# Inverse transform of the long convolution with the spectra as stationary operand, in a fused float32 block pair

## The chip, the cores and the metric

The kernel runs on one core of one Trainium2 chip. The metric is the device time of one execution in microseconds (us). TensorE is called PE, its weight loads PEld, VectorE DVE, ScalarE ACT, GpSimd POOL, SyncE SP. Everything is computed in float32: most products go as three products of rounded parts (hi times hi, hi times lo, lo times hi), the transform below as plain float32 matrix products, which the chip splits in two records each.

## What is computed

Two blocks follow each other on 1024 tokens of 1024 channels: a Hyena block (long convolution and SwiGLU), then a block with gated linear attention and pooling. The change lies in the long convolution:

```python
z = short_conv(u @ w_in + b_in, conv_w, conv_b)
x0, x1, v = jnp.split(z, 3, axis=-1)
s = (v * x1).astype(jnp.float32)
g = hyena_filter(L, ...)
n = 2 * L
y = jnp.fft.irfft(jnp.fft.rfft(s, n=n, axis=1) * jnp.fft.rfft(g, n=n, axis=0)[None],
                  n=n, axis=1)[:, :L]
y = (y + s * skip.astype(jnp.float32)).astype(u.dtype) * x0
return y @ w_out + b_out
```

## The kernel before

Activations lie with channels on partitions, in 8 tiles of 128 channels by 1024 tokens. The Fourier transform of the convolution is split into a part over 16 positions and a part over 64 (of 128): 16 groups of spectra are multiplied and transformed back over the 16 positions in the stage "spec" (`inverse`, `spec_inverse`). Each of its 32 half steps ends with a copy of a result by ACT to `yi` (L1438) and a transfer of 256 KB from ACT's DMA queue into `YB` (L1441): even steps bring channels 0 to 511 (semaphore `yb_in[0]`), odd steps channels 512 to 1023 (`yb_in[1]`). `YB` is 128 partitions (64 frequencies, real and imaginary) by 16 positions by 1024 channels.

The stage "inv" does the rest, by a list `INV` of 24 jobs, each with one of the four PSUM tiles `ps` of 128 x 1024 in turn:

- a "rows" job (16 of them) multiplies the 128 x 64 matrix `idft`, as stationary operand, with 1024 columns of `YB` (L1233), in pieces of 512 columns for channels 0 to 511 (8 jobs) and of 256 columns for the others. The result has 64 partitions (time) and goes back into `YB` by an ACT copy (L1503).
- a "tile" job (8, one for each 128 channels) transposes those rows with 16 small transposes of 64 x 128 (L1238), so that channels are on partitions.

DVE then makes of each tile e: `y` = `ps` * `rn` + skip term (L1914), times the gate `G0` (L1919), and, one tile behind, the low part `A[:, 1, e]` (`y_lo_of`, L1904). ACT makes the skip term (`skip_of`, L1487) and the high part (`y_hi_of`, L1481). The output projection "wout" follows on PE (`panel_mm`, L1060): 8 jobs, each of 8 steps k of 6 products of 512 columns, and its first job waits at step k for the low part of tile k (`y_lo`).

The order on every engine is that of the program text; engines meet by semaphores. Before "inv", PE waits for `spec_ev`, the last copy to `yi`, and for `yb_in`. SP loads the block's input `X` (4 MB) again as soon as PE, ACT and DVE have ended "spec" (L943).

Of the kernel before, what the change touches and what calls it, by code (L numbers as in the profile page):

```python
# [20 lines left out]
ACT = mybir.ActivationFunctionType  # L21
# [3 lines left out]
P = 128  # L25
D = 1024
T = 1024
KT = D // P
# [10 lines left out]
N1, N2 = 128, 16  # L39
HALF = N1 // 2  # L40
GROUPS = 16
# [26 lines left out]

INV = [("rows", 0, 512, n2) for n2 in range(0, N2, 2)]
for _e in range(4):
    INV += [("rows", 512, 256, 4 * _e), ("tile", _e)]
INV += [("rows", 768, 256, 0), ("tile", 4)] + [("rows", 768, 256, _n2) for _n2 in (4, 8, 12)]
INV += [("tile", _e) for _e in (5, 6, 7)]


def inv_rows(e):

    return max(o for o, j in enumerate(INV) if j[0] == "rows" and j[1] <= 128 * e < j[1] + j[2])  # L80

PHASES = [("mlp0", 1, 0), ("zin0", 1, 1), ("norm1", 1, 0), ("zin1", 1, 1), ("mlp1", 1, 0), ("zin2", 1, 1),
          ("mlp2", 1, 0), ("zin3", 1, 1), ("zin4", 12, 12), ("mix", 40, 8), ("sfwd", 32, 0), ("tapnorm", 1, 0),
          ("spec", 0, GROUPS), ("inv", len(INV), 0), ("wout", 8, 8), ("first", 1, 1), ("norm2", 1, 0), ("second", 3, 3)]


UPS = [[(f"up{_p}", _n // 2)] for _p, _n in enumerate(FPARTS)]
# [11 lines left out]
J0, N0, A0 = {}, {}, {}  # L101
_j = _n_ = 0
for _name, _jobs, _pan in PHASES:
# [5 lines left out]
assert V_PANEL % 2 == 0 and HP % 2 == 0  # L109

_a = 0
AUX = {"norm1": 1, "mlp0": 1, "mlp1": 1, "mlp2": 1, "mix": 32, "tapnorm": 1, "sfwd": 32, "inv": len(INV), "norm2": 1,
       "normf": 1, "normc": 1, "lr": 1, "heads": HA * HEADS, "pool": 8, "norm4": 1}
for _name, _, _ in PHASES:
    A0[_name] = _a
# [29 lines left out]
def program(nc, d, out):  # L145

    ctx = ExitStack()
    with ctx:
# [38 lines left out]
        TT = [at(f"T{i}", [P, T], RT + 4 * K * i) for i in range(4)]  # L187
# [45 lines left out]
        YB = at("YB", [P, N2, T], RH)  # L233
# [41 lines left out]
        ps = [ctx.enter_context(nc.psum_tensor(f"ps{s}", [P, 2 * 512], F32)) for s in range(4)]  # L275
# [17 lines left out]
        panel_done, aux_done = sem("panel_done"), sem("aux_done")  # L293
        evac = [sem(f"evac{s}") for s in range(4)]
# [3 lines left out]
        def slot(phase, u):  # L298
            return (J0[phase] + u) % 4

        def turn(phase, u, i=0, per=0):

            return (J0[phase] + u) // 4 + i * (per // 4)
# [28 lines left out]
        n1, n2 = NormSems("mix", tiles=False), NormSems("ffn", tiles=False)  # L332
# [29 lines left out]
        yb_in = [sem("yb_in0"), sem("yb_in1")]  # L362
# [31 lines left out]
        def cc(name, rows=P):  # L394
            w = {"idft": 64, "tneg": 16, "tmask": 16}.get(name, 128)
            return cst[0:rows, CST[name]:CST[name] + w]

        ident, ones = cc("ident"), cc("ones")
# [640 lines left out]
        def _(pe):  # L1039
            mm = nc.tensor.matmul  # L1040

            def free(phase, u, i=0, per=0):

                q = turn(phase, u, i, per)
                if not (isinstance(q, int) and q == 0):
                    pe.wait_ge(evac[slot(phase, u)], q)
# [78 lines left out]
            with pe.Fori(0, 2) as i:  # L1125
                for q in range(4):
                    o, g = 5 * q, i * 4 + q
# [7 lines left out]
                    for u in range(2):  # L1135
                        p = begin(1 + u)
                        pe.wait_ge(hbs_made, g * 2 + (u + 1))
                        for c in range(2):
                            last = mm(p[:, c * 512:(c + 1) * 512], hbs[u][:, :], wtap[:, c * 512:(c + 1) * 512],
                                      start=True, stop=True)  # L1140
                        last.then_inc(aux_done, 1)
                    for u in range(2):
                        p = begin(3 + u)

                        pe.wait_ge(evac[slot("mix", o + 1 + u)], turn("mix", o + 1 + u, i, 20) + 1)
                        for c in range(2):
                            last = mm(p[:, c * 512:(c + 1) * 512], cc("dft_g"), tap[u][:, c * 512:(c + 1) * 512],
                                      start=True, stop=True)
                        last.then_inc(aux_done, 1)

            with pe.Fori(0, N2 // 2) as i:
                for u in range(2):
# [3 lines left out]
                    for e in range(KT):  # L1156
                        last = nc.tensor.transpose(ps[slot("sfwd", u)][0:HALF, e * P:(e + 1) * P], sn[u][:, e, :], ident)
                    last.then_inc(aux_done, 1)
                for u in range(2):
                    free("sfwd", 2 + u, i, 4)  # L1160
                    pe.wait_ge(evac[slot("sfwd", u)], turn("sfwd", u, i, 4) + 1)
                    for c in range(2):
                        last = mm(ps[slot("sfwd", 2 + u)][:, c * 512:(c + 1) * 512], cc("dft_s", HALF),
                                  st_[u][:, c * 512:(c + 1) * 512], start=True, stop=True)
# [3 lines left out]
            for e in range(KT):  # L1168
                last = mm(ps[slot("tapnorm", 0)][:, e:e + 1], gacc[:, e * P:(e + 1) * P], ones[:, 0:1],
                          start=True, stop=True)  # L1170
# [41 lines left out]
            for n in range(2 * GROUPS):  # L1212
                g, c = n // 2, n % 2
# [8 lines left out]
            pe.drain().then_inc(ended["pe"], 1)  # L1222

            pe.wait_ge(spec_ev, 2 * GROUPS)
            for o, (kind, *j) in enumerate(INV):
                p = ps[slot("inv", o)]
                free("inv", o)
                if kind == "rows":
                    c0, w, m0 = j
                    if m0 == 0:  # L1230
                        pe.wait_ge(yb_in[c0 // 512], 16 * GROUPS)
                    for u in range(T // w):
                        last = mm(p[0:HALF, u * w:(u + 1) * w], cc("idft"), YB[:, m0 + u, c0:c0 + w], start=True, stop=True)  # L1233
                else:
                    e, q = j[0], inv_rows(j[0])
                    pe.wait_ge(evac[slot("inv", q)], turn("inv", q) + 1)
                    for m in range(N2):
                        last = nc.tensor.transpose(p[:, m * HALF:(m + 1) * HALF], YB[0:HALF, m, e * P:(e + 1) * P],  # L1238
                                                   ident[0:HALF, 0:HALF])
                last.then_inc(aux_done, 1)  # L1240
            panel_jobs("wout", 2, A, ready=(y_lo, 0))
            project("first", 0, (n2.lo, 0))
# [35 lines left out]
            for g in range(4):  # L1278
# [6 lines left out]
                for m in range(2):  # L1285
                    free("pool", 6 * g + 4 + m)
                    for k in range(2):
                        pe.wait_ge(pd_made, 2 * g + k + 1)
                        for c in range(2):
                            last = mm(ps[slot("pool", 6 * g + 4 + m)][:, c * 512:(c + 1) * 512],  # L1290
                                      wpl[:, k, m * P:(m + 1) * P], pd[k][:, c * 512:(c + 1) * 512],
                                      start=(k == 0), stop=(k == 1))
# [9 lines left out]
        def _(act):  # L1302
            A_ = nc.scalar.activation
# [157 lines left out]
            for n in range(2 * GROUPS):  # L1461
                c = n % 2
# [16 lines left out]
            def y_hi_of(e):  # L1479
                act.wait_ge(y_made, e + 1)  # L1480
                A_(A[:, 0, e, :], TT[2 + e % 2][:, :], ACT.Copy).then_inc(y_hi, 1)  # L1481

            def skip_of(e):
                if e >= 2:
                    o = INV.index(("tile", e - 2))
                    act.wait_ge(evac[slot("inv", o)], turn("inv", o) + 1)
                A_(TT[e % 2][:, :], S[:, e, :], ACT.Copy, scale=vcol("skip", e)).then_inc(skip_made, 1)  # L1487

            def around(e):

                if e:
                    y_hi_of(e - 1)
                    if e + 1 < KT:
                        skip_of(e + 1)

            skip_of(0)
            skip_of(1)
            for o, (kind, *j) in enumerate(INV):
                if kind == "rows":

                    c0, w, m0 = j
                    act.wait_ge(aux_done, A0["inv"] + o + 1)
                    A_(YB[0:HALF, m0:m0 + T // w, c0:c0 + w], ps[slot("inv", o)][0:HALF, :].rearrange("p (a b) -> p a b", b=w),  # L1503
                       ACT.Copy).then_inc(evac[slot("inv", o)], 1)

                    if o and INV[o - 1][0] == "tile":
                        around(INV[o - 1][1])
                elif o + 1 == len(INV) or INV[o + 1][0] == "tile":
                    around(j[0])
            y_hi_of(KT - 1)  # L1510

            def residual_squares(ph, n, src, gain=None):
# [31 lines left out]
            for p, nf in enumerate(FPARTS):  # L1544
                last = p == len(FPARTS) - 1
# [17 lines left out]
            with act.Fori(0, 2) as i:  # L1563
                for u in range(4):
                    e = i * 4 + u
# [47 lines left out]
            with act.Fori(0, 2) as i:  # L1613
                for u in range(4):
                    e = i * 4 + u
# [5 lines left out]
            for g in range(4):  # L1621
# [4 lines left out]
                for u in range(2):  # L1626
                    s = slot("pool", 6 * g + u)
                    act.wait_ge(panel_done, N0["pool"] + 4 * g + u + 1)
                    A_(up[u][:, PAD:PAD + T], ps[s][:, :], ACT.Copy).then_inc(evac[s], 1)
                for m in range(2):  # L1630
                    s = slot("pool", 6 * g + 2 + m)
# [6 lines left out]
            with act.Fori(0, 2) as i:  # L1638
                for u in range(4):
                    e = i * 4 + u  # L1640
# [36 lines left out]
        def _(dve):  # L1677
# [137 lines left out]
            with dve.Fori(0, 3) as i:  # L1815
                ch.enter(i, 8 + 8 + 1)
                for u in range(4):
                    z_tile(slot("zin4", u), turn("zin4", u, i, 4) + 1, i * 4 + (N0["zin4"] + u),
                           i * 2 + (10 + 8 * (u % 2) + u // 2))
                    for j in range(2):  # L1820
                        m = 2 * u + j
# [9 lines left out]
                    n, e = i * 4 + (N0["zin4"] + u), i * 2 + (2 + u // 2)  # L1831
# [9 lines left out]
            with dve.Fori(0, 2) as i:  # L1841
                ch.enter(i, 16)
                for q in range(4):
                    o, g = 5 * q, i * 4 + q
                    z_tile(slot("mix", o), turn("mix", o, i, 20) + 1, g + N0["mix"], g)
                    for u in range(2):
                        s = slot("mix", o + 1 + u)
# [3 lines left out]
                    for u in range(2):  # L1851
                        s = slot("mix", o + 1 + u)
# [34 lines left out]
            for n in range(2 * GROUPS):  # L1887
                c = n % 2
# [16 lines left out]
                                 ).then_inc(y_lo, 1)  # L1905

            for e in range(KT):
                o = INV.index(("tile", e))
                s, y = slot("inv", o), TT[2 + e % 2]
                dve.wait_ge(skip_made, e + 1)  # L1910
                if e >= 2:
                    dve.wait_ge(y_lo, e - 1)
                dve.wait_ge(aux_done, A0["inv"] + o + 1)
                V_.scalar_tensor_tensor(out=y[:, :].rearrange("p (a b) -> p a b", b=N2),  # L1914
                                        in0=ps[s][:, :].rearrange("p (b a) -> p a b", a=HALF),
                                        scalar=rn[:, e:e + 1], in1=TT[e % 2][:, :].rearrange("p (a b) -> p a b", b=N2),
                                        op0=ALU.mult, op1=ALU.add).then_inc(evac[s], 1)
                dve.wait_ge(evac[s], turn("inv", o) + 1)
                V_.tensor_tensor(y[:, :], y[:, :], G0[:, e, :], ALU.mult).then_inc(y_made, 1)  # L1919
                if e:  # L1920
                    y_lo_of(e - 1)
# [350 lines left out]
```

## Time and profile before

| | us |
|---|---|
| median of 3 runs | 2643.86 |
| lowest and highest run | 2642.76, 2653.99 |
| span of the profiled execution | 2636.2 |
| stage "inv" on PE in it, first product to the first of "wout" | 635.3 to 674.7 |
| busy PE / DVE / ACT over the span | 94% / 44% / 25% |

The span is the time from the first to the last instruction of the profiled execution; the metric has some 7.7 us more around it. Times in rows are us from the span's start unless marked ns.

### The profile page before, as it was taken

The page shows a single profiled execution, that of the slowest core. Times are in us where ns is not written, and L with a number is a line of the kernel's source. Part 1 is how long each engine was busy: PE and PEld are TensorE (multiplying, and loading weights), DVE is VectorE, ACT ScalarE, POOL GpSimd, SP SyncE. Part 2 cuts the span into 40 slices and gives each one's busy share as a digit, 9 for nine tenths or more (in the row PEclk, how much of TensorE's full clock was granted, in tenths as well). Part 3 has the DMA queues.
Part 4 walks back from the last instruction along what each step waited for, and adds up shares of the span by engine and source line. Part 5 has one row for each costly group of instructions (what it writes and reads, how often), then busy time and mean ns, then how long its engine had stood idle before and what let it go on. Part 6 is the DMA issues. An engine that isn't in the chain of part 4 may idle for free.

```text
span 2636.2 us, 29935 instructions
## 1 busy us (share of the span) xinstructions
PE 2482.3 (94%) x11420; PEld 1987.5 (75%) x11420; DVE 1164.5 (44%) x1221; ACT 661.1 (25%) x816; POOL 702.4 (27%) x394
## 2 busy tenths in 40 slices
PE   7987998777999999999999889999999999999996
PEld 5775665444788888888888679888888787778885
DVE  7899564332623321331234693626262322430443
ACT  4102345344411000010012262626363101111011
POOL 2233111331232333333333312222212232233331
PEclk9998999898999999999999899999999999999998
DMA  5232215876011111111111120202011421111231
GB/s 190 73 127 88 80 64 209 162 169 146 24 48 48 48 48 48 48 49 52 66 48 48 56 96 25 72 24 72 27 69 47 187 90 59 64 40 57 95 120 72
DMA packets 61099, 208.06 MB, mean 79 GB/s; under 512 B 6182, under 2 KB 7848, under 8 KB 60906
## 3 DMA queue, kind: packets, MB, share of 16 engines
q1 hardware_dynamic: 46090, 161.02, 18.8%
q10 hardware_dynamic: 14944, 46.14, 5.9%
q8 instruction: 45, 0.74, 0.1%
q14 instruction: 20, 0.16, 0.0%
HBM read 162.05 MB, written 36.70 MB: 75 GB/s over the span
## 4 chain that ended last, share of the span: by engine, by line
PE 70%; DVE 3%; ACT 1%; issue 0%; ACTq 0%; DVEq 0%
PE ps L1060 59%; PE ps L468 4%; DVE T L1687 1%; PE ps L1290 1%; PE ps L515 1%; PE ps L534 1%; PE ps L497 1%; PE ps L536 1%; PE ps L535 1%; PE ps L1082 0%; DVE XN L1717 0%; PE ps L1091 0%; DVE X L1997 0%; DVE H L1710 0%; PE ps L439 0%; DVE T L1717 0%
## 5 line engine op out<-in xcount | busy, mean ns | idle before, releaser
L1060 PE MATMUL ps<-H,whi 128*128 128x512 f32 x4000 | 1086.3, 394 | 32.9 <-POOL wlo L1016 14.0
L1060 PEld LDWEIGHTS ps<-H,whi 128*128 128x128 f32 x4000 | 752.6, 189 | 204.9 <-issue 23.7
L1014 POOL CAST whi<-wraw 128x1024 fp32r<-128x1024 f32 x190 | 201.5, 1060 | 1808.2 <-issue 738.8
L1060 PE MATMUL ps<-H,wlo 128*128 128x512 f32 x2000 | 619.3, 391 | 0.0
L1016 POOL TENSOR_TENSOR wlo<-wraw,whi 128x1024 fp32r<-128x1024 f32 x194 | 489.0, 2521 | 58.5 <-ACT whi L602 43.3
L1060 PEld LDWEIGHTS ps<-H,wlo 128*128 128x128 f32 x2000 | 377.2, 189 | 79.3
L1060 PE MATMUL ps<-A,whi 128*128 128x512 f32 x1472 | 395.6, 391 | 6.4 <-DVE A L2029 4.9
L1060 PEld LDWEIGHTS ps<-A,whi 128*128 128x128 f32 x1472 | 277.0, 189 | 65.0 <-issue 5.3
L1060 PE MATMUL ps<-A,wlo 128*128 128x512 f32 x736 | 227.0, 390 | 0.0
L1060 PEld LDWEIGHTS ps<-A,wlo 128*128 128x128 f32 x736 | 138.6, 188 | 28.9
L1946 DVE TENSOR_TENSOR T<-ps,T 128x1024 f32<-128x1024 f32 x22 | 26.9, 1224 | 202.6 <-PE ps L1060 202.6
L1538 ACT ACTIVATE A<-T 128x1024 f32 (+1 forms) x22 | 23.3, 1061 | 280.0 <-DVE T L1949 280.0
L1997 DVE TENSOR_TENSOR X<-ps,X 128x1024 f32 x24 | 29.4, 1225 | 144.6 <-PE ps L1060 142.5
L1824 DVE CUSTOM_DVE_ANT_0 mprod<-mw,crep 128x1024 f32<-128x1024 f32 x48 | 86.9, 1810 | 2.5 <-DVE zp L1787 1.0
L1687 DVE TENSOR_TENSOR T<-T,T 128x1024 f32<-128x1024 f32 x40 | 69.4, 1734 | 23.1 <-ACT T L1524 11.5
L1949 DVE TENSOR_TENSOR T<-T,T 128x1024 f32<-128x1024 f32 x22 | 72.3, 3285 | 3.9 <-ACT T L1535 1.4
L1535 ACT ACTIVATE T<-T 128x1024 f32<-128x1024 f32 x22 | 23.4, 1062 | 201.6 <-DVE T L1944 201.6
L468 PE MATMUL ps<-whi,H 128*128 128x256 f32 x512 | 64.4, 284 | 5.8 <-ACT whi L602 5.8
L468 PEld LDWEIGHTS ps<-whi,H 128*128 128x128 f32 x512 | 62.5, 192 | 6.6 <-issue 6.6
L1894 DVE TENSOR_TENSOR ya<-ps,ga 128x512 f32<-128x512 f32 x32 | 22.1, 691 | 102.0 <-ACT ga L1466 86.7
L1944 DVE TENSOR_TENSOR T<-ps,T 128x1024 f32<-128x1024 f32 x22 | 26.9, 1225 | 84.7 <-PE ps L1060 73.5
L2077 DVE TENSOR_TENSOR T<-X,ps 128x1024 f32<-128x1024 f32 x8 | 9.8, 1221 | 119.6 <-PE ps L1060 119.6
(342 smaller groups left out, 2614.3 us busy)
## 6 DMA issues: line engine op xcount, KB each, us to landing
wraw<-in_panels SPq DMA_DIRECT2D x181, 512.0 KB, 3.4
mw<-in_modp SPq DMA_DIRECT2D x24, 512.0 KB, 3.5
g<-gsp ACTq DMA_DIRECT2D x16, 512.0 KB, 2.6
wraw<-g SPq DMA_DIRECT2D x16, 512.0 KB, 11.1
s<-sa SPq DMA_DIRECT2D x16, 512.0 KB, 2.6
bs<-s SPq DMA_DIRECT2D x16, 512.0 KB, 7.8
YB<-yi ACTq DMA_DIRECT2D x32, 256.0 KB
kf<-in_kfft SPq DMA_DIRECT2D x16, 320.0 KB, 8.2
```

The source lines that it names most:

```text
L468: last = mm(p(u)[:, t * DV:(t + 1) * DV], operand(act, a, k, (t0 + t) * P, P), w[:, :, k, :], start=(k == 0 and a == 0 and w is whi), stop ...
L497: last = mm(chunk(p(14 + dr), c), chunk(KD[dr], c), chunk(QD[dr], c), start=True, stop=True)
L515: last = mm(p(u)[:, (c % 4) * DV:(c % 4 + 1) * DV], KDT[dr][:, c, :], V[:, c, :], start=True, stop=True)
L1014: nc.gpsimd.tensor_copy(whi[:, s, :, :], wraw[:, s, :, :]).then_inc(hi_made, 1)
L1016: nc.gpsimd.tensor_tensor(wlo[:, s, :, :], wraw[:, s, :, :], whi[:, s, :, :].bitcast(F32), ALU.subtract).then_inc(split_made, 1)
L1060: last = mm(p[:, c * step:(c + 1) * step], w[:, ws, k, :], operand(act, a, k, c * step, step), start=(q == 0 and w is whi and a == 0), sto ...
L1687: V_.tensor_tensor(acc, acc, tile, ALU.add).then_inc(n.acc, 1)
L1824: i_ = V_.tensor_tensor_reduce(mprod[:, :], mw[m % 4][:, :], crep[:, w * D:(w + 1) * D], 1.0, 0.0, ALU.mult, ALU.add, macc[:, m, w:w + 1])
L1944: V_.tensor_tensor(TT[0][:, :], ps[gs][:, :], TT[3][:, :], ALU.mult).then_inc(evac[gs], 1)
L1946: V_.tensor_tensor(TT[2][:, :], ps[us][:, :], TT[3][:, :], ALU.mult).then_inc(evac[us], 1)
L1949: V_.tensor_tensor(TT[2][:, :], TT[2][:, :], TT[0][:, :], ALU.mult).then_inc(ff_prod, 1)
L1997: V_.tensor_tensor(x, ps[slot(ph, u)][:, :], x, ALU.add).then_inc(evac[slot(ph, u)], 1)
```

## The change

"inv" has 8 jobs in place of 24. A job is one tile of 128 channels: 16 products, each with `YB[:, m, e]` (128 frequencies x 128 channels) as stationary operand and `idft` (64 columns) as moving operand. The result stands with channels on partitions at once. The 16 rows jobs, the 16 ACT copies and the 128 transposes are gone. The first job waits for both halves of `YB`. DVE's operations on a tile are unchanged.

```diff
-            for o, (kind, *j) in enumerate(INV):
-                p = ps[slot("inv", o)]
-                free("inv", o)
-                if kind == "rows":
-                    c0, w, m0 = j
-                    if m0 == 0:
-                        pe.wait_ge(yb_in[c0 // 512], 16 * GROUPS)
-                    for u in range(T // w):
-                        last = mm(p[0:HALF, u * w:(u + 1) * w], cc("idft"), YB[:, m0 + u, c0:c0 + w], start=True, stop=True)
-                else:
-                    e, q = j[0], inv_rows(j[0])
-                    pe.wait_ge(evac[slot("inv", q)], turn("inv", q) + 1)
-                    for m in range(N2):
-                        last = nc.tensor.transpose(p[:, m * HALF:(m + 1) * HALF], YB[0:HALF, m, e * P:(e + 1) * P],
-                                                   ident[0:HALF, 0:HALF])
+            for e in range(KT):
+                free("inv", e)
+                if e == 0:
+                    for c in range(2):
+                        pe.wait_ge(yb_in[c], 16 * GROUPS)
+                for m in range(N2):
+                    last = mm(ps[slot("inv", e)][:, m * HALF:(m + 1) * HALF], YB[:, m, e * P:(e + 1) * P], cc("idft"),
+                              start=True, stop=True)
                 last.then_inc(aux_done, 1)
...
-            for o, (kind, *j) in enumerate(INV):
-                if kind == "rows":
-
-                    c0, w, m0 = j
-                    act.wait_ge(aux_done, A0["inv"] + o + 1)
-                    A_(YB[0:HALF, m0:m0 + T // w, c0:c0 + w], ps[slot("inv", o)][0:HALF, :].rearrange("p (a b) -> p a b", b=w),
-                       ACT.Copy).then_inc(evac[slot("inv", o)], 1)
-
-                    if o and INV[o - 1][0] == "tile":
-                        around(INV[o - 1][1])
-                elif o + 1 == len(INV) or INV[o + 1][0] == "tile":
-                    around(j[0])
+            for e in range(1, KT):
+                y_hi_of(e - 1)
+                if e + 1 < KT:
+                    skip_of(e + 1)
             y_hi_of(KT - 1)
```

PE of the kernel before, from the last job on channels 0 to 511 on (`evac` are the semaphores of the four `ps`, `cst` holds `idft` and the identity; "128x64" is the result):

```order
L1233 MATMUL ps<-YB,cst 64x512 [waits evac0]
L1233 MATMUL ps<-YB,cst 64x512
L1233 MATMUL ps<-YB,cst 64x256 [waits yb_in1,evac1]
L1233 MATMUL ps<-YB,cst 64x256 x3
L1238 MATMUL ps<-cst,YB 128x64 [waits evac0,evac2]
L1238 MATMUL ps<-cst,YB 128x64 x15
L1233 MATMUL ps<-YB,cst 64x256 [waits evac3]
L1233 MATMUL ps<-YB,cst 64x256 x3
```

PE of the changed kernel, from the end of "spec" on:

```order
L1174 MATMUL ps<-yb_126,kf_106 128x512 [waits spec_y]
L1218 MATMUL ps<-cst,YB 128x64 [waits yb_in0,yb_in1,evac1,spec_ev]
L1218 MATMUL ps<-cst,YB 128x64 x15
L1218 MATMUL ps<-cst,YB 128x64 [waits evac2]
L1218 MATMUL ps<-cst,YB 128x64 x15
```

The wait for `yb_in1` stood behind eight jobs and now stands ahead of the first; each of the 8 jobs issues 16 products with 64 moving columns.

ACT of the kernel before, at the end of "spec" and in "inv":

```order
L1438 ACTIVATE yi_128<-ps 128x512 [waits yb_in1,spec_inv]
L1441 DMA YB<-yi_128 8x16x512 [waits spec_ev]
L1487 ACTIVATE T_66<-S,vec 128x1024 [waits ended_dve,ended_pe]
L1487 ACTIVATE T_67<-S,vec 128x1024
L1503 ACTIVATE YB<-ps 64x2x512 [waits aux_done] x8
```

ACT of the changed kernel at the same place:

```order
L1418 ACTIVATE yi_128<-ps 128x512 [waits yb_in1,spec_inv]
L1421 DMA YB<-yi_128 8x16x512 [waits spec_ev]
L1466 ACTIVATE T_66<-S,vec 128x1024 [waits ended_dve,ended_pe]
L1466 ACTIVATE T_67<-S,vec 128x1024
L1461 ACTIVATE A<-T_68 128x1024 [waits y_made]
```

The copies into `YB` are gone and nothing came in their place; the last transfer into `YB` is issued where it was.

## Rows read from the trace of the kernel before

**Rows 1.** The page, part 1: busy time, share, instructions of three engines.
```profile
PE 2482.3 (94%) x11420; PEld 1987.5 (75%) x11420; DVE 1164.5 (44%) x1221; ACT 661.1 (25%) x816; POOL 702.4 (27%) x394
```

**Rows 2.** Chain of waits, 560 to 760: start, us, what.
```profile
684.40 75.78 PE ps L1060 x333
```

**Rows 3.** Stages: us, busy (x) of PE, PEld, DVE, ACT, POOL, granted clock, DMA, GB/s.
```profile
635.20:638.20 3.00, 2.89 (x4) 0.98 (x5) 0.00 (x0) 0.00 (x0) 0.00 (x0) 0.50 1.09 89
638.30:652.30 14.00, 14.00 (x37) 4.80 (x35) 0.00 (x0) 8.14 (x8) 0.00 (x0) 1.00 0.95 355
652.30:674.60 22.30, 21.90 (x185) 15.84 (x184) 18.62 (x16) 17.86 (x18) 0.00 (x0) 1.00 0.01 1
```

**Rows 4.** Timeline around the stage's start: start, us, engine, line, idle before.
```profile
621.47 0.62 ACTq L1441 DMA_DIRECT2D YB<-yi  x1
...
627.75 0.62 ACTq L1441 DMA_DIRECT2D YB<-yi  x1
...
630.06 0.60 ACT L1438 ACTIVATE yi<-ps 128x512 f32<-128x512 f32 x1 [2.34 <-DMA YB<-yi]
630.68 0.62 ACTq L1441 DMA_DIRECT2D YB<-yi  x1
632.02 0.40 SPq L943 DMA_DIRECT2D X<-in_xT  x1
...
635.31 17.11 PE L1233 MATMUL ps<-YB,cst 128*64 128x512 f32 x40 [5.98 <-DMA YB<-yi]
```

**Rows 5.** ACT's DMA queue, 635.3 to 640.6: packets, MB, share.
```profile
q10 hardware_dynamic: 68, 0.12, 29.4%
```

**Rows 6.** DMA queues, 639 to 645, all that moved: packets, MB, share.
```profile
q1 hardware_dynamic: 535, 2.19, 99.8%
```

**Rows 7.** Groups by shape: stationary, moving or out<-in, xcount | busy, mean ns.
```profile
L534 PE MATMUL ps<-T,V 128*128 128x128 f32 x128 | 24.7, 275 | 0.0
...
L1503 ACT ACTIVATE YB<-ps 64x1024 f32<-64x1024 f32 x16 | 16.2, 1017 | 14.1 <-PE ps L1233 14.0
```

**Rows 8.** Timeline of PE, 1592 to 1599: products of 128 moving columns.
```profile
1595.30 1.95 PE L497 MATMUL ps<-QF,KF 128*128 128x128 f32 x16
1597.09 1.95 PE L497 MATMUL ps<-QT,KT 128*128 128x128 f32 x16
```

**Rows 9.** Timeline of PE, 1480 to 1520: after a pause of 9.8 us.
```profile
1496.68 6.96 PE L1082 MATMUL ps<-cst,T 128*128 128x1 f32 x32 [9.81 <-DVE T L1687]
1503.51 0.56 PE L1060 MATMUL ps<-HCH,whi 128*128 128x256 f32 x1
```

**Rows 10.** Stages there, columns as in rows 3.
```profile
1496.70:1503.50 6.80, 6.80 (x32) 6.80 (x33) 1.10 (x1) 0.85 (x1) 0.00 (x0) 0.50 0.00 0
1503.60:1508.60 5.00, 5.00 (x25) 5.00 (x25) 1.20 (x7) 1.72 (x3) 0.00 (x0) 0.50 0.00 0
1508.80:1512.00 3.20, 3.20 (x31) 3.20 (x31) 1.29 (x2) 0.00 (x0) 0.00 (x0) 1.00 0.00 0
```

**Rows 11.** Timeline of PE, 2618 to 2624, at the low clock.
```profile
2619.29 3.79 PE L1091 MATMUL ps<-cst,nr 128*128 128x128 f32 x16 [2.83 <-DVE nr L1696]
```

**Rows 12.** Timeline of DVE, 660 to 687: the last tiles.
```profile
676.89 1.28 DVE L1914 SCALAR_TENSOR_TENSOR T<-ps,rn,T 128x1024 f32<-128x1024 f32 x1
...
680.66 1.28 DVE L1914 SCALAR_TENSOR_TENSOR T<-ps,rn,T 128x1024 f32<-128x1024 f32 x1
...
683.12 2.43 DVE L1904 TENSOR_TENSOR A<-T,A 128x1024 fp32r<-128x1024 f32 x2
```

**Rows 13.** Timeline of PE, 674 to 690: the first job of "wout" and the next.
```profile
674.66 1.20 PE L1060 MATMUL ps<-A,whi 128*128 128x512 f32 x4
...
680.24 1.07 PE L1060 MATMUL ps<-A,whi 128*128 128x512 f32 x4
...
681.60 1.07 PE L1060 MATMUL ps<-A,whi 128*128 128x512 f32 x4
...
687.26 1.07 PE L1060 MATMUL ps<-A,whi 128*128 128x512 f32 x4
```

More of the change, by code:

```diff
@@ L67 @@
 NCST = _c
[L71 to L80, printed above, removed]
 PHASES = [("mlp0", 1, 0), ("zin0", 1, 1), ("norm1", 1, 0), ("zin1", 1, 1), ("mlp1", 1, 0), ("zin2", 1, 1),
           ("mlp2", 1, 0), ("zin3", 1, 1), ("zin4", 12, 12), ("mix", 40, 8), ("sfwd", 32, 0), ("tapnorm", 1, 0),
-          ("spec", 0, GROUPS), ("inv", len(INV), 0), ("wout", 8, 8), ("first", 1, 1), ("norm2", 1, 0), ("second", 3, 3)]
+          ("spec", 0, GROUPS), ("inv", KT, 0), ("wout", 8, 8), ("first", 1, 1), ("norm2", 1, 0), ("second", 3, 3)]
 UPS = [[(f"up{_p}", _n // 2)] for _p, _n in enumerate(FPARTS)]
@@ L111 @@
 _a = 0
-AUX = {"norm1": 1, "mlp0": 1, "mlp1": 1, "mlp2": 1, "mix": 32, "tapnorm": 1, "sfwd": 32, "inv": len(INV), "norm2": 1,
+AUX = {"norm1": 1, "mlp0": 1, "mlp1": 1, "mlp2": 1, "mix": 32, "tapnorm": 1, "sfwd": 32, "inv": KT, "norm2": 1,
        "normf": 1, "normc": 1, "lr": 1, "heads": HA * HEADS, "pool": 8, "norm4": 1}
@@ L1484, in skip_of @@
                 if e >= 2:
-                    o = INV.index(("tile", e - 2))
-                    act.wait_ge(evac[slot("inv", o)], turn("inv", o) + 1)
+                    act.wait_ge(evac[slot("inv", e - 2)], turn("inv", e - 2) + 1)
                 A_(TT[e % 2][:, :], S[:, e, :], ACT.Copy, scale=vcol("skip", e)).then_inc(skip_made, 1)
[L1489 to L1494, printed above, removed]
             skip_of(0)
             skip_of(1)
-            for o, (kind, *j) in enumerate(INV):
-                if kind == "rows":
-                    c0, w, m0 = j
-                    act.wait_ge(aux_done, A0["inv"] + o + 1)
-                    A_(YB[0:HALF, m0:m0 + T // w, c0:c0 + w], ps[slot("inv", o)][0:HALF, :].rearrange("p (a b) -> p a b", b=w),
-                       ACT.Copy).then_inc(evac[slot("inv", o)], 1)
-                    if o and INV[o - 1][0] == "tile":
-                        around(INV[o - 1][1])
-                elif o + 1 == len(INV) or INV[o + 1][0] == "tile":
-                    around(j[0])
+            for e in range(1, KT):
+                y_hi_of(e - 1)
+                if e + 1 < KT:
+                    skip_of(e + 1)
             y_hi_of(KT - 1)
@@ L1907, in _ @@
             for e in range(KT):
-                o = INV.index(("tile", e))
-                s, y = slot("inv", o), TT[2 + e % 2]
+                s, y = slot("inv", e), TT[2 + e % 2]
                 dve.wait_ge(skip_made, e + 1)
@@ L1912, in _ @@
                     dve.wait_ge(y_lo, e - 1)
-                dve.wait_ge(aux_done, A0["inv"] + o + 1)
+                dve.wait_ge(aux_done, A0["inv"] + e + 1)
                 V_.scalar_tensor_tensor(out=y[:, :].rearrange("p (a b) -> p a b", b=N2),
@@ L1917, in _ @@
                                         op0=ALU.mult, op1=ALU.add).then_inc(evac[s], 1)
-                dve.wait_ge(evac[s], turn("inv", o) + 1)
+                dve.wait_ge(evac[s], turn("inv", e) + 1)
                 V_.tensor_tensor(y[:, :], y[:, :], G0[:, e, :], ALU.mult).then_inc(y_made, 1)
```

## The prediction, made before the changed kernel was run

> **What bounds the kernel now.** I read the page first: PE is busy for 94% of the span, DVE for 44% and ACT for 25% [rows 1], so the question is always what PE does and when it stands. The chain of waits around the place of the change shows PE from 684.40 on without a break [rows 2]. The table of stages then shows "inv" in three pieces: 3.0 us at the low clock (granted share 0.50, that is 1.2 GHz), 14.0 us of rows jobs at the high one (2.4 GHz), and 22.3 us of rows and transposes mixed, in which PE is busy for 21.9 [rows 3]. ACT is busy for 17.9 us of the last piece, but PE hardly waits for it: the copies that go are beside PE's work. PE is the bound of the stage, from its first product at 635.31 [rows 4] to the first of "wout" at 674.66 [rows 13], 39.4 us. Everything behind is PE's too, so what PE gains or loses here reaches the end.
>
> **Start of the stage.** PE stands idle from the end of "spec" and begins when the first half of `YB` is there: its last transfer is issued at 627.75, PE starts at 635.31, 7.5 us later [rows 4]. The change makes the first job wait for the second half too. That is issued at 630.68 [rows 4] and nobody waits for it before, so its landing must be bounded. Its own predecessor in that half took from 621.47 to 630.06, 8.6 us [rows 4]. With 7.5 to 8.6 us it would land at 638.2 to 639.3; from 632.02 on it shares the DMA engines with the 4 MB of `X` [rows 4]. ACT's queue still moved 68 packets between 635.3 and 640.6 [rows 5], and none from 639 on [rows 6]. So not before 638.2, and with the completion behind the last packet perhaps 642. I take 640.0, close behind the last packet: **4.7 us later** (2.9 to 6.7) than 635.3. What hides this now is eight rows jobs on the first half; that cover is gone. Queued behind the waiting product on PE is the whole of "inv" and "wout"; DVE and ACT wait with it, having nothing else.
>
> **The products.** 8 tiles x 16 products, each plain float32 with 128 x 128 stationary: two records each, as `L534` shows, which the program issues 64 times and the trace lists 128 times [rows 7]. That makes 256 records, each with a weight load of 128 columns and 64 moving columns. No such shape is in the trace; the nearest are the same load with 128 and with 1 moving columns, and they bound it from both sides:
> - high clock: 16 records of 128 moving columns start 1595.30, the next 16 at 1597.09 [rows 8]: 1.79 / 16 = 0.112 us a record;
> - low clock: 32 records of 1 moving column from 1496.68 to 1503.51 [rows 9]: 6.83 / 32 = 0.213 us. With 128 moving columns 16 records show as 3.79 us [rows 11]; the 16 at the high clock show as 1.95 for a pace of 1.79 [rows 8], a tail of 0.16, twice that at half the clock, so (3.79 - 0.32) / 16 = 0.217 us.
>
> At the low clock 1 and 128 columns cost nearly the same (0.213 and 0.217), so the load sets the pace and 64 columns cost it too: there is no discount for the small moving operand. I take the 0.213 of the longer run and keep 0.217 as the upper end. The stage is 256 x 0.112 = 28.7 us at the high clock and 256 x 0.2134 = **54.6 us** at the low one, against 39.4 before. Which clock it gets decides the sign.
>
> The Trainium skill ("TensorE: Matmul & The Clock Gate", section "LDWEIGHTS (loading the stationary operand)") gives columns / 1.2 in ns with no word on the clock, 107 ns for 128 columns. The rows agree at the high clock (112 ns a record) and not at the low one (213 ns). By the page the stage would be about 27 us at either clock; the measurement decides.
>
> **The clock.** PE enters at the low level: it is at 0.50 when "inv" starts before, after a pause of 6 us [rows 3, 4], and the pause now grows by 4.7. Before, the stage begins with products of 512 moving columns and the clock is up 3.0 us later [rows 3]. After, it begins with loads of 128 columns and only 64 columns to move. The trace has one long run of that kind from the low clock: the 32 records with 1 moving column, PE and PEld busy for all of 6.8 us, and the clock stayed at 0.50; it rose only after 5.0 us of the 256-column products behind them [rows 10]. So a PE that is busy does not always get the high clock: before both rises PE did products of 256 or 512 columns, and what it did without a rise were short products whose time is weight load. The new stage is of that second kind, load-bound in every one of its records as those 32 are, and the same from its first record to its last. I take the case that is nearest to it: **it stays at 1.2 GHz to its end**.
>
> **Behind the stage.** "inv" ends at 640.0 + 54.6 = 694.6, 19.9 us later than 674.7. DVE needs 680.66 - 676.89 = 3.77 us a tile [rows 12] and PE 32 x 0.213 = 6.8, so DVE waits for PE at each tile and is no bound. Behind the last tile it does L1914, L1919 and two L1904 (680.66 to 685.55, 4.9 us [rows 12]), done at about 699.6, while PE needs the low parts of tiles 6 and 7 only after six steps of "wout" (681.60 - 680.24 = 1.36 us each at the high clock [rows 13], 8.2 us). So the stall goes that now stands before step 6, which starts at 684.40 [rows 2]: from step 5 at 681.60, three steps of 1.36 would bring the second job to 685.7, and it starts at 687.26 [rows 13], **-1.6 us**. In its place "wout" now starts at the low clock. Its operand is 512 columns wide and lifts the clock after 3 to 5 us [rows 3, 10], half of which is lost: **+2.0 us** (1.5 to 2.6). The 16 copies of ACT (1.02 us each [rows 7], under PE's work) bring nothing more.
>
> Sum: +4.7 of waiting, 54.6 - 39.4 = +15.2 of products, -1.6, +2.0: **+20.3 us**. The profiled execution has a span of 2636.2 and would have 2656.5; the median lies 7.7 above its span, so 2643.9 + 20.3 = **2664.2 us**. Own range of this case: landing -1.8 / +2.0, pace 0 / +1.0, lift of the clock -0.5 / +0.6, and a few us by which medians of this kernel move (runs 2642.8 to 2654.0): 2659 to 2669.
>
> **Rivals.**
> - The clock rises in the stage. If these products lift it as the 512-column ones did, it rises 3 to 5 us after the start, say 4 (half of which is lost): 28.7 + 2.0 = 30.7 us, end at 670.7, 4.0 earlier; DVE, from tile 1 at 649 on with 3.77 a tile, makes its last low part at 677, ahead of step 7 at 680.2; the stall of 1.6 goes as well. -5.6 us: **2638.3**. For it speaks that the products are longer than those of 1 column; against it the 6.8 busy us at 0.50 [rows 10]. The Trainium skill (same page, "Part 1: The HAM clock gate") is on this side: sustained matmul work lifts the clock, and "The HW doesn't count instructions"; the time by it is that of this rival. The 32 records above do not agree.
> - The clock rises late in the stage. With half of the records at each pace the products take 27.3 + 14.3 = 41.6 us, +2.2; with the landing and without the stall, +5.3: **2649.2**.
> - The second half of `YB` lands with `X` and not ahead of it, at 650: 10 us more than forecast, **2674**. Before, PE took it at about 649 to 651 with no wait; against it, queue 10 is silent after 639 [rows 6].
> - The change does what it says: the rows of PE's order show 16 products a tile and no copies; I see no case in which it does not.
>
> **How the numbers follow.** Low clock throughout 0.80, clock rises 0.11, halfway 0.06, late landing 0.03. About 0.5% (13.2 us) is what a measurement of this kernel can tell from no change: slower means over 2657.1. The forecast and the late landing are slower, 0.83 less 0.01 for a forecast that falls short; the others are within 0.5% (0.17), with 0.01 for a gain beyond. The range takes the forecast's own and reaches some us towards both neighbours: 2655 to 2671.
>
> **What would show it.** Right: the first product of "inv" at about 640 waiting for the DMA into `YB`; granted clock 0.50 over the whole stage; 32 records a tile in 6.8 us; DVE's L1914 starts 6.8 us apart; no wait of "wout" for L1904; the clock up some 3 us into "wout". Wrong: a granted clock of 1.00 from about 644 on and 3.6 to 3.8 us a tile is the first rival; a start after 642 means the transfer was mis-sized.

## The result: 0.7% slower, as forecast, and where the time went

| | before | changed |
|---|---|---|
| median, us | 2644.36 (4 runs) | 2664.07 (4 runs) |
| lowest, highest | 2642.76, 2653.99 | 2659.38, 2668.37 |
| span of the profiled execution | 2636.2 | 2657.6 |

The ratio of the times is 1.007 (95% interval 1.0053 to 1.0087): slower by 0.5% to 0.9%. The forecast was 2664.2 us; the medians of four sets of runs of the kernel before lie between 2643.5 and 2647.3 us, so an agreement to 0.1 us is luck.

The timeline of the changed kernel around the start of the stage (start, us, engine, line, what; in brackets the idle time before and what ended it), to be held against [rows 4]:

```profile
627.73 0.62 ACTq L1421 DMA_DIRECT2D YB<-yi  x1
631.37 0.60 ACT L1418 ACTIVATE yi<-ps 128x512 f32<-128x512 f32 x1 [3.67 <-DMA YB<-yi]
631.99 0.62 ACTq L1421 DMA_DIRECT2D YB<-yi  x1
...
641.37 6.85 PE L1218 MATMUL ps<-cst,YB 128*128 128x64 f32 x31 [13.23 <-DMA YB<-yi]
```

PE now stands idle for 13.2 us and is released by the transfer into `YB` that was issued at 631.99, 9.4 us before. The next view is PE's timeline to the second job of "wout":

```profile
641.37 54.85 PE L1218 MATMUL ps<-cst,YB 128*128 128x64 f32 x256 [13.23 <-DMA YB<-yi]
695.97 2.05 PE L1047 MATMUL ps<-A,whi 128*128 128x512 f32 x4
...
709.15 1.07 PE L1047 MATMUL ps<-A,whi 128*128 128x512 f32 x4
```

These are 256 records, without a gap among them, from 641.37 to 695.97. The table of stages (columns as in [rows 3]; the share behind the five pairs is the granted clock) says at which clock:

```profile
629.30:641.30 12.00, 0.00 (x0) 0.00 (x0) 0.00 (x0) 2.78 (x3) 0.00 (x0) 0.63 0.79 99
641.40:695.90 54.50, 54.50 (x256) 54.50 (x256) 24.37 (x20) 13.63 (x13) 0.00 (x0) 0.50 0.20 84
696.00:700.50 4.50, 4.50 (x13) 3.53 (x13) 4.11 (x4) 1.06 (x1) 0.00 (x0) 0.50 0.00 0
700.70:709.00 8.30, 8.30 (x38) 6.83 (x37) 1.46 (x2) 0.00 (x0) 0.00 (x0) 1.00 0.01 2
```

PE and its weight loads are busy for all of 54.5 us and the clock is 0.50 (1.2 GHz) for all of it. It is up only 4.6 us into the wide products of "wout". In before, the same stage had the high clock for all but its first 3 us [rows 3].

DVE's last tiles, to be held against [rows 12]:

```profile
689.52 1.28 DVE L1877 SCALAR_TENSOR_TENSOR T<-ps,rn,T 128x1024 f32<-128x1024 f32 x1 [3.15 <-PE ps L1218]
...
696.35 1.28 DVE L1877 SCALAR_TENSOR_TENSOR T<-ps,rn,T 128x1024 f32<-128x1024 f32 x1 [3.15 <-PE ps L1218]
697.67 1.22 DVE L1882 TENSOR_TENSOR T<-T,G 128x1024 f32<-128x1024 f32 x1
698.81 2.43 DVE L1868 TENSOR_TENSOR A<-T,A 128x1024 fp32r<-128x1024 f32 x2
```

A tile comes every 6.83 us and DVE waits 3.15 us for each. Its last low part is done at 701.2, while "wout" is still at its third step: no wait is left there.

From the profiles, then: the first product starts 6.1 us later (641.37 against 635.31), the products take 54.6 in place of 39.4 us (+15.2), and "wout"'s first job 13.2 in place of 12.6 (+0.6: the stall of [rows 13] is gone, the low clock is paid in its place). That is +21.9 at the second job; the spans differ by 21.4. The chain of waits of the changed kernel (start, us, what) reads the same way:

```profile
631.99 9.24 DMA YB<-yi
641.23 0.14 issue
641.37 54.85 PE ps L1218 x256
696.22 63.87 PE ps L1047 x272
```

### The profile page after: what moved, and what is told of

Read it like the earlier page. It is cut to its first block, busy times and chain, and to the rows that moved or that the text cites. A ratio compares the mean times of both kernels' runs of the same rounds, so it can differ in the third digit from the quotient of the medians.

```text
span 2657.6 us, 29974 instructions
## 1 busy us (share of the span) xinstructions
PE 2501.9 (94%) x11452; PEld 2024.5 (76%) x11452; DVE 1164.3 (44%) x1221; ACT 646.2 (24%) x800; POOL 703.7 (26%) x394
## 4 chain that ended last, share of the span: by engine, by line
PE 79%; DVE 8%; DMA 6%; issue 4%; ACT 2%; DVEq 0%; ACTq 0%; SPq 0%
PE ps L1047 63%; DMA YB<-yi 5%; PE ps L455 4%; PE ps L1218 2%; DVE T L1651 1%; PE ps L1134 1%; PE ps L1150 1%; PE ps L1270 1%; DVE zp L1751 1%; PE ps L502 1%; PE ps L522 1%; PE ps L484 1%; PE ps L521 1%; PE ps L523 1%; PE ps L1069 1%
## 5 line engine op out<-in xcount | busy, mean ns | idle before, releaser
L1047 PEld LDWEIGHTS ps<-H,whi 128*128 128x128 f32 x4000 | 753.1, 189 | 204.5 <-issue 23.6
L1909 DVE TENSOR_TENSOR T<-ps,T 128x1024 f32<-128x1024 f32 x22 | 26.9, 1224 | 202.6 <-PE ps L1047 202.6
L1218 PE MATMUL ps<-cst,YB 128*128 128x64 f32 x256 | 54.8, 421 | 13.2 <-DMA YB<-yi 13.2
L1218 PEld LDWEIGHTS ps<-cst,YB 128*128 128x128 f32 x256 | 54.7, 333 | 14.0 <-issue 14.0
```

Of the source, the lines that this page charges most:

```text
L1047: last = mm(p[:, c * step:(c + 1) * step], w[:, ws, k, :], operand(act, a, k, c * step, step), start=(q == 0 and w is whi and a == 0), sto ...
L1218: last = mm(ps[slot("inv", e)][:, m * HALF:(m + 1) * HALF], YB[:, m, e * P:(e + 1) * P], cc("idft"), start=True, stop=True)
L1909: V_.tensor_tensor(TT[2][:, :], ps[us][:, :], TT[3][:, :], ALU.mult).then_inc(evac[us], 1)
```

## The experiments

Theory: the stage loses because it is entered at the low clock and its products, bound by weight loads, do not lift it. First rival: a record of this shape costs 0.213 us whatever the clock. Second: any busy PE gets the high clock, and only the pause hurts. Third: the longer wait is the main loss. In all diffs below the changed kernel is the base, but for the one that says otherwise. The kernel before ran again beside each group of experiments, and a ratio is to those runs. So two experiments of different groups are better compared by their ratios than by their times.

**More columns, same loads.** The `idft` columns have 64 others ahead of them in `cst`. With those as part of the moving operand, 14 of the 16 products of a tile (all but m = 0 and 8) write 64 columns too many, and the next product, in descending order of m, overwrites them.

```diff
-                for m in range(N2):
-                    last = mm(ps[slot("inv", e)][:, m * HALF:(m + 1) * HALF], YB[:, m, e * P:(e + 1) * P], cc("idft"),
-                              start=True, stop=True)
+                for m in reversed(range(N2)):
+                    extra = 0 if m % 8 == 0 else HALF
+                    last = mm(ps[slot("inv", e)][:, m * HALF - extra:(m + 1) * HALF], YB[:, m, e * P:(e + 1) * P],
+                              cst[:, CST["idft"] - extra:CST["idft"] + HALF], start=True, stop=True)
```

> The changed kernel with the moving operand widened from 64 to 128 columns in 14 of the 16 products of a tile: the 64 columns ahead of the inverse matrix go along, and what they make is overwritten by the next product. The same 256 weight loads, more columns, the same result. Theory (weight loads set the pace at either clock, and longer moving operands lift the clock): the clock rises 3 to 5 us into the stage, a record then costs 0.112 us, the stage takes 28.7 + 2 = 31 us: 2664.1 - 24 - 2 = 2638 us, faster although PE does more. Rival (the pace of 0.213 us does not hang on the clock): 2664 us. Rival (moving columns add to the loads): over 2664 us.

Measured: 2636.58 us (6 runs, 2634.46 to 2638.85), ratio to before 0.9968 (0.9952 to 0.9985). PE's timeline of the stage, its stages, then PE's timeline at the start of "wout":

```profile
642.99 31.20 PE L1219 MATMUL ps<-cst,YB 128*128 128x128 f32 x256 [12.86 <-DMA YB<-yi]
```

```profile
643.00:648.00 5.00, 5.00 (x23) 5.00 (x24) 0.00 (x0) 0.00 (x0) 0.00 (x0) 0.50 1.02 422
648.20:673.90 25.70, 25.70 (x233) 25.70 (x232) 22.89 (x19) 12.58 (x12) 0.00 (x0) 1.00 0.23 93
```

```profile
674.00 1.17 PE L1047 MATMUL ps<-A,whi 128*128 128x512 f32 x4
```

23 records in 5.0 us at 0.50, that is 0.217 us each; 233 in 25.7 us at 1.00, 0.110 us each. The stage takes 674.0 - 643.0 = 31.0 us in place of 54.6, for almost twice the columns. The first rival falls: the pace follows the clock. With 64 moving columns the clock stayed low to the end, with 128 it was up after 5 us; PE was busy without a gap in both kernels, with the same loads, and stood idle for as long ahead of them (12.9 and 13.2 us). The 128-column records, too, cost no more than a few per cent over the load's own time at the low clock (0.217 against 0.213 us) and yet the clock rose: being bound by the load is not what keeps it low. The edit also reverses the order of m; the order was not varied by itself.

**Filling the pause.** Four runs put plain products (results thrown away, extra work) between the end of "spec" and the stage. This is the diff of the first; the others differ in number and width.

```diff
+            pe.wait_ge(spec_ev, 2 * GROUPS - 1)
+            for q in range(12):
+                mm(ps[0][:, 512 * (q % 2):512 * (q % 2) + 512], ident, S[:, q % 8, 0:512], start=True, stop=True)
             pe.wait_ge(spec_ev, 2 * GROUPS)
```

> The changed kernel with 12 plain float32 products of 512 moving columns (24 records, result thrown away) put into PE's pause ahead of the inverse stage, where it waits 13.2 us for the transfer into YB. Theory (the stage runs at the low clock because it is entered at the low clock and its own short products do not lift it): granted clock 1.00 in the whole stage, 0.112 us a record, 28.7 us in place of 54.6, and the projection behind it starts at the high clock: 2664.1 - 25.9 - 2.0 = 2636 us. Rival (a record of this shape costs 0.213 us at any clock): 2664 us. Rival (the clock falls back inside the stage): between, 2640 to 2660 us, with a change of the granted clock inside the stage.

Measured: 2664.07 us (4 runs, 2658.80 to 2666.41), ratio 1.0061 (1.0044 to 1.0078). Not the 2636 of the theory. Timeline of PE and of its weight loads (PEld, whose idle time is counted from the last load; PE's own is 3.4 us), and the stages:

```profile
632.90 10.57 PE L1213 MATMUL ps<-S,cst 128*128 128x512 f32 x24
...
646.83 15.44 PEld L1221 LDWEIGHTS ps<-cst,YB 128*128 128x128 f32 x72 [4.19 <-issue]
```

```profile
642.30:645.60 3.30, 1.17 (x3) 0.19 (x1) 0.00 (x0) 0.00 (x0) 0.00 (x0) 1.00 1.04 89
645.80:701.00 55.20, 54.14 (x254) 54.17 (x255) 24.37 (x20) 13.63 (x13) 0.00 (x0) 0.50 0.22 89
```

The 24 records ran at the high clock and ended at 643.5, but this execution reached the stage some 5 us later than the profiled one of the changed kernel, from which I had taken their number. PE stood some 3.4 us more before the transfer landed at 646.8, the clock fell in that gap, and the stage ran at 0.50 to its end. The forecast of 2636 missed because the filling was too short; the run says nothing against the theory, and one thing for it: a gap of 3.4 us ahead of the stage is enough to lose the high clock for all of it.

> As e1_prewarm, but the pause is filled with 28 products of 64 moving columns (56 records, the shape of the stage itself), so PE is as busy as there. Theory (products whose time is weight load do not lift the clock): the clock falls or stays low all the same and the stage takes 54.6 us: 2664 us (2660 to 2668). Rival (any busy PE gets the high clock, what hurts is the pause alone): 2636 to 2640 us. Should the clock not fall before the stage begins, the stage would keep it: then 2636 too, and the trace tells the two apart by whether the clock rose or never fell.

Measured: 2671.21 us (4 runs, 2669.07 to 2673.98), ratio 1.0095 (1.0078 to 1.0111). The short products ended at 640.5 and left a gap of 6.4 us; the stage took 54.6 us again, at the low clock:

```profile
641.80:701.20 59.40, 54.33 (x255) 54.36 (x256) 24.37 (x20) 13.63 (x13) 0.00 (x0) 0.50 0.27 88
```

It therefore tells the second rival apart no better than e1. That it is some 7 us slower than e1 was not expected: both profiles start "wout" at 701.47, and the spans are 2670.2 and 2664.6. Three parts are visible. In "wout"'s first job the clock rises later: the third step starts at 706.64 here and at 705.37 in e1. And at two later places PE ran the same kind of work at 0.50 in this kernel and at 1.00 in e1. First this kernel, then e1, at the second of these places:

```profile
1959.30:1962.50 3.20, 3.20 (x9) 2.42 (x9) 1.15 (x2) 3.17 (x4) 0.82 (x1) 0.50 0.60 243
```

```profile
1958.30:1961.50 3.20, 3.20 (x15) 2.63 (x14) 2.96 (x4) 3.17 (x4) 1.25 (x1) 1.00 0.18 55
```

15 records against 9 in the same 3.2 us, at each of the two places. Why the clock fell there in one kernel and not in the other stays open.

The two runs were repeated with enough products to reach the landing, 17 wide ones and 60 short ones.

> As e1_prewarm, with 17 in place of 12 products of 512 columns. In e1 they ended 3.6 us before the transfer landed and the clock had fallen when the stage began. Now they reach to the landing. Theory: the stage is entered at the high clock and, with its 64 moving columns unchanged, keeps it: 28.7 us, 2664 - 26 - 2 = 2636 us. Rival (the stage's own products do not hold the clock either): it falls inside the stage, 2655 to 2664 us.

Measured: 2637.49 us (4 runs, 2633.31 to 2638.59), ratio 0.9955 (0.9937 to 0.9973). Timeline of PE and stage:

```profile
632.21 14.85 PE L1213 MATMUL ps<-S,cst 128*128 128x512 f32 x34
646.90 28.69 PE L1221 MATMUL ps<-cst,YB 128*128 128x64 f32 x256
```

```profile
647.00:675.50 28.50, 28.50 (x258) 28.50 (x257) 23.08 (x19) 12.57 (x12) 0.00 (x0) 1.00 0.32 131
```

The stage with its 64 columns unchanged, entered at the high clock, keeps it and takes 28.5 us (646.90 to 675.41). Entered at the low one it takes 54.6. "wout", which here starts at the high clock, needs 11.0 us for its first job in place of 13.2. The two make 28.3 us; the times differ by 26.6 us, and by 29.5 when each is held against its own runs of the kernel before. No other cause is needed.

> As e8_prewarm_long, with the pause filled by 60 products of 64 moving columns. The products before the pause leave the clock high. If short products hold a clock that is high and only fail to raise one that is low, the stage is entered high and takes 28.7 us: 2636 to 2638 us. If they do not hold it, the clock falls among them, and the stage runs at the low clock: 2664 us or more. I expect the first.

Measured: 2639.67 us (10 runs, 2632.89 to 2648.32), ratio 0.9972 (0.9958 to 0.9986). Its timeline of PE and its stages:

```profile
633.45 13.61 PE L1213 MATMUL ps<-S,cst 128*128 128x64 f32 x120
647.43 28.77 PE L1221 MATMUL ps<-cst,YB 128*128 128x64 f32 x256 [0.36 <-DMA YB<-yi]
```

```profile
633.50:647.00 13.50, 13.50 (x120) 13.43 (x120) 0.00 (x0) 2.78 (x3) 0.89 (x1) 1.00 0.76 85
647.50:676.00 28.50, 28.50 (x256) 28.50 (x257) 22.98 (x19) 12.57 (x12) 0.00 (x0) 1.00 0.39 159
```

120 short records of 0.113 us and the stage behind them ran at the high clock from end to end. The same shape that does not raise a low clock in 54 us holds a high one for 42 us. The second rival falls in its simple form: in these runs being busy with this shape was enough to hold the clock, and (the changed kernel's own 54.5 busy us at 0.50) not enough to raise it.

**The wait.** One run takes the wait for the second half away from the first tile (to the second, the latest place that keeps DVE's writes to `T` off the transfer's source, which shares memory with `T`), one puts it into the kernel before.

```diff
-                if e == 0:
-                    for c in range(2):
-                        pe.wait_ge(yb_in[c], 16 * GROUPS)
+                if e < 2:
+                    pe.wait_ge(yb_in[e], 16 * GROUPS)
```

> The changed kernel with the wait for the second half of YB moved from the first tile to the second. Theory: the first product starts when the first half lands, some 5 us earlier, tile 0 takes 6.8 us at the low clock, the second half has landed by then; nothing else changes: 2664.1 - 5 = 2659 us, the clock still 0.50 over the stage. Rival (the start is not on the path, something behind the stage is late): 2664 us.

Measured: 2660.52 us (5 runs, 2657.56 to 2673.58), ratio 1.0061 (1.0037 to 1.0086). The direction fits (3.6 us below the changed kernel, 5 expected), but the interval of the ratio holds the changed kernel's 1.007, so the times support no more than "a few us, not the main loss". In its profile PE stands 6.4 us for the transfer in place of 13.2, and the stage is again 0.50 throughout:

```profile
641.90 20.50 PE L1217 MATMUL ps<-cst,YB 128*128 128x64 f32 x95 [6.44 <-DMA YB<-yi]
```

In the kernel before:

```diff
                     if m0 == 0:
-                        pe.wait_ge(yb_in[c0 // 512], 16 * GROUPS)
+                        for c in range(2):
+                            pe.wait_ge(yb_in[c], 16 * GROUPS)
```

> The kernel before, with the first rows job waiting for both halves of YB as the changed kernel does. Theory: this wait alone costs the 4.7 to 5.5 us by which the second half lands later (2645 + 5 = 2650 us); the rows jobs lift the clock as before. Rival (the transfers overlap with something that is late anyway): 2645 us.

Measured: 2653.93 us (10 runs, 2647.22 to 2658.20), ratio 1.002 (1.0009 to 1.0031), that is +5.3 us (2.4 to 8.2) on 2647; the medians lie 6.6 apart. The wait alone costs about what the theory says and is a quarter to a third of the loss: the third rival falls.

```profile
645.81 17.93 PE L1234 MATMUL ps<-YB,cst 128*64 128x512 f32 x40 [12.91 <-DMA YB<-yi]
```

This run settles one thing more. It enters the stage behind a pause as long as the changed kernel's (12.9 against 13.2 us), at 0.50, and its products of 512 columns had the clock back within 5 us (0.50 until 650.0, a mean of 0.98 from 650 to 663). So the length of the pause is not what kept the clock low in the changed kernel.

**Together.**

> e3_wide (128 moving columns in 14 of 16 products) and e4_split (the second tile waits for the second half of YB) together. Theory: both effects add, since one is the start and the other the pace: 2636.6 - 4 = 2632 us, the clock up 3 to 5 us after the first product. Rival: DVE, which needs 3.77 us a tile against 3.58 on PE, or the pause between tile 0 and tile 1 eats the gain: 2636 us.

Measured: 2634.49 us (4 runs, 2632.78 to 2637.86), ratio 0.9946 (0.993 to 0.9963). Of the 4 us expected on top of e3 2.1 came by the times and 5.8 by the ratios; the intervals of the two overlap, so the size is not resolved. In its profile, too, the clock comes back within the stage, after about 6 us:

```profile
642.20:648.00 5.80, 5.80 (x27) 5.80 (x28) 0.00 (x0) 0.00 (x0) 0.00 (x0) 0.50 0.99 151
648.20:673.70 25.50, 25.50 (x231) 25.50 (x230) 23.09 (x19) 12.58 (x12) 0.00 (x0) 1.00 0.41 168
```

> The changed kernel with 10 products of 512 columns in the pause (up to the landing of the first half of YB) and the wait for the second half at the second tile. The moving operand stays at 64 columns. Theory: the stage starts some 5 us earlier than in e8_prewarm_long and at the high clock; tile 0 takes 3.6 us, then PE waits 1 to 2 us for the second half, too short for the clock to fall: 2637.5 - 3.5 = 2634 us or a little less. Rival (the clock falls in that pause or the one before, and nothing lifts it again): about 2655 us.

Measured: median 2651.29 us, but in two groups: 5 of 11 executions at 2627.9 to 2632.8, 6 at 2651.3 to 2662.1. Both the theory (2634 or a little less) and its rival (about 2655) came, each in about half of the executions. The profiled one is of the first group: 20 wide records end at 640.7, the stage goes on without a gap and at the high clock, with 0.34 us of waiting between tile 0 and tile 1:

```profile
640.58 3.68 PE L1220 MATMUL ps<-cst,YB 128*128 128x64 f32 x32
644.60 25.20 PE L1220 MATMUL ps<-cst,YB 128*128 128x64 f32 x224 [0.34 <-DMA YB<-yi]
```

The mean granted clock of the executions is 0.976 to 0.978 in the first group and 0.965 to 0.970 in the second. The medians of the groups lie 26.2 us apart, the stages of 54.6 and 28.5 us 26.1. I read this as the clock that fell ahead of the stage in about half of the executions and was not raised again; no profile of the second group was taken, so it is inferred from the times and the mean clock.

> e10_split_prewarm with the 128 moving columns of e3_wide. Theory: at the high clock both widths cost the load's 0.112 us, so it equals e10 where the clock holds, and it gets the clock back where it falls: 2632 to 2634 us. Rival (more columns cost time at the high clock): above e10 by up to 1 us or more.

Measured: 2634.45 us (11 runs, 2627.18 to 2642.66), ratio 0.9967 (0.9951 to 0.9983). The same kernel with 128 moving columns has no second group. That the clock falls in some of its executions too and comes back within the stage is inferred from e3 and e7, where it did; the profiled execution of e11 is one in which it did not fall. At the high clock the extra columns cost nothing: 224 records take 25.20 us in both profiles.

```profile
643.40 25.20 PE L1221 MATMUL ps<-cst,YB 128*128 128x128 f32 x224 [0.90 <-DMA YB<-yi]
```

The best versions, e3, e7, e8, e9 and e11, are 0.3 to 0.5% faster than the kernel before and do not differ clearly among themselves. e3 is the least edit.

## Why the prediction was right

- **Start of the stage.** Forecast 640.0 and 4.7 us later. Measured 641.37, 6.1 later; the transfer took 9.4 us from its issue to PE's start (forecast 9.3). The rest is that "spec" itself ended 1.3 us later in this execution. This term was 1.4 us short. e5 isolates the wait: +5.3 us.
- **Pace.** Forecast 0.2134 us a record and 54.6 us for the stage, measured 54.60 / 256 = 0.2133. Taking the row with 1 moving column for a stage with 64 was right: 1, 64 and 128 moving columns cost 0.213, 0.213 and 0.217 us at the low clock, so the load sets the pace.
- **Clock.** 0.50 over the whole stage, as forecast with a chance of 0.80. e3 and e8 show that the clock is the cause. The reason given was too wide, though. The prediction put the stage beside the 32 records of 1 column because both are load-bound; e3's records of 128 columns are load-bound as well (0.217 us) and did lift the clock. No row of before told whether 64 columns go with 1 or with 128, so this step was a judgement that came true. Why the stage with 128 columns lifted the clock and the one with 64 did not stays open. The first rival's price was sound: e3, where the clock does rise, has 2636.6 us against its 2638.3.
- **By the Trainium skill** ("TensorE: Matmul & The Clock Gate", "Part 1: The HAM clock gate"), sustained work would have lifted the clock; 54.5 us of work without a gap did not. Its load time for 128 columns (section "LDWEIGHTS (loading the stationary operand)", 107 ns) holds at the high clock (0.110 to 0.112 us) and not at the low one (0.213 us).
- **Behind the stage.** -1.6 and +2.0 forecast, +0.6 together measured, where the sum gives +0.4. No stall on L1868; the clock up after 4.6 us, within the 3 to 5 assumed.
- **The sum** was +20.3, the profiles show +21.4, the medians +19.7. The terms are right to 1.6 us; that the medians come closer still is luck.
- **A slip that did no harm.** I took the 7.7 us between the median and the span of before for time around the span. The changed kernel's profiled execution has 2659.38 us for a span of 2657.6: only 1.8 us lie around it, and 1.7 to 2.1 in every other execution on record. With as much around its span of 2636.2, the profiled execution of before was simply a fast one, about 6 us under its median; that of the changed kernel is 4.7 under its own.

In the experiments the misses were e1 and e2. For both the number of filling products was read from one execution, and in e1's "spec" ended 4.6 us later; e2 came out above its forecast of 2660 to 2668 us as well, in part for a cause that stays open.

## What to carry to other kernels

Swapping the operands of small products trades wide moving operands for weight loads. Count the weight loads, take their price at both clocks, and ask at which clock the stage is entered: behind a pause it can stay at half speed to its end, however busy PE looks. If so, widen the moving operand with columns that are overwritten later: 128 in place of 64 brought the clock back here and cost nothing at the high clock. Filling the pause works too, but only if it reaches almost to the landing in every execution: gaps of 0.3 to 0.9 us did no harm here, one of 3.4 us did.

## What the runs showed of the hardware that I had not expected

- The granted clock has memory in this stage. The same 256 records ran at 1.00 for 28.5 us when entered high (e8, e9) and at 0.50 for 54.6 us when entered low.
- The stage with 128 moving columns, 0.217 us a record at the low clock and 0.110 at the high one, is 23.6 us shorter than with 64 when both are entered at the low clock.
- The last transfers of 256 KB to 8 partitions take 7.5 to 9.4 us from issue to landing ([rows 4] and the changed kernel), and earlier ones longer, up to 11.1 us in the changed kernel's chain of waits. They lead the chain at the end of "spec": from 560 to 760 they are 34.4% of the time. The line of the chain view that sums it up says where a next gain would be looked for, and the longest transfer stands below it:

```profile
by line: DMA YB<-yi 34.4%; PE ps L1047 31.9%; PE ps L1218 27.4%; ACT yi L1418 2.1%; DVE bl L1845 1.1%; PE ps L1174 0.9%; issue 0.5%; DVE ya L1858 0.3%; ACTq L1421 0.3%; ACT ga L1446 0.3%; DVE yb L1858 0.3%; PE ps L1181 0.3%; PE ps L1183 0.1
603.26 11.07 DMA YB<-yi
```
